# Removing two groups of discarded products from the router stage of a transformer-block kernel

## The reference

```
h = rms_norm(x, norm2_g[l]) * (1.0 + sc2) + sh2
...
logits = (xt @ router_w + router_b).astype(jnp.float32)
top_v, top_e = lax.top_k(logits, TOP_K)          # 4 of 32 experts for each token
gate = jax.nn.softmax(top_v, axis=-1)
...
hb = xb @ w1[e] + b1[e]                          # xb: the tokens of expert e
glu = g * jax.nn.sigmoid(g * SWIGLU_ALPHA)
return ((u + 1.0) * glu) @ w2[e] + b2[e]
```

## Time and profile before

| | |
|---|---|
| median of 3 runs | 2230.92 us (2228.34 to 2231.58) |
| the profiled execution's own time | 2230.52 us |
| its span | 2228.7 us |
| mean granted clock of TensorE | 0.972 |
| PE busy | 2094.6 us (94%) |
| DVE, ACT busy | 701.0 us (31%), 448.4 us (20%) |
| kernel start to the last attention product (L1494) | about 406.5 us |
| router stage, to the first product of expert 0 (L1749) | 406.5 to 442.35 us |
| expert loop | 442.35 to about 1435 us |

### The profile page before, as it was taken

The page is one execution under the profiler, slowest core; times in us unless marked ns, Lnnn a source line. Parts: engine busy times, 40 slices in busy tenths (PEclk is TensorE's granted clock), DMA queues, the critical chain, the costliest instruction groups (busy, mean ns, idle before and its releaser), DMA issues.

```text
span 2228.7 us, 28718 instructions
## 1 busy us (share of the span) xinstructions
PE 2094.6 (94%) x10964; PEld 1204.8 (54%) x10965; DVE 701.0 (31%) x1479; ACT 448.4 (20%) x874; POOL 0.2 (0%) x4
## 2 busy tenths in 40 slices
PE   6999989899989999999999999899999999999997
PEld 3767757433333333333333333376489976648996
DVE  2333223311110111111111111214267753525776
ACT  1322230100000000000000000112245431114543
POOL 0000000000000000000000000000000000000000
PEclk9999989899989999999999999999999999999999
DMA  9254674499978999999999979963166645432652
GB/s 357 89 172 167 227 195 149 186 376 426 424 282 338 425 425 426 425 426 425 426 425 426 424 274 426 366 164 104 29 187 181 184 127 144 139 104 86 196 171 84
DMA packets 189021, 590.95 MB, mean 265 GB/s; under 512 B 10571, under 2 KB 110466, under 8 KB 152996
## 3 DMA queue, kind: packets, MB, share of 16 engines
q1 hardware_dynamic: 186940, 587.68, 70.0%
q10 hardware_dynamic: 2024, 2.46, 0.4%
HBM read 587.48 MB, written 2.62 MB: 265 GB/s over the span
## 4 chain that ended last, share of the span: by engine, by line
PE 76%; DMA 17%; DVE 3%; ACT 2%; issue 1%; SPq 0%; ACTq 0%; DVEq 0%
DMA lower<-in_exp_w 16%; PE psum L1756 15%; PE psum L1941 11%; PE psum L1407 7%; PE psum L1780 6%; PE psum L1953 5%; PE psum L1509 5%; PE psum L1514 5%; PE psum L1541 3%; PE psum L1488 2%; PE psum L1800 2%; PE psum L1724 2%; PE psum L1494 1%; PE psum L1415 1%; PE psum L1749 1%
## 5 line engine op out<-in xcount | busy, mean ns | idle before, releaser
L1756 PE MATMUL psum<-lower,upper 128*64 128x512 f32 x2176 | 487.6, 602 | 25.6 <-DMA lower<-in_exp_w 25.6
L1756 PEld LDWEIGHTS psum<-lower,upper 128*64 128x64 f32 x2176 | 150.9, 137 | 362.4 <-issue 308.2
L1941 PEld LDWEIGHTS psum<-rounded 128*128 128x128 f32 x2112 | 258.6, 189 | 3.4
L1941 PE MATMUL psum<-rounded 128*128 128x256 f32 x2112 | 260.1, 283 | 0.0
L1780 PE MATMUL psum<-upper 128*64 128x512 f32 x1088 | 240.5, 595 | 6.8 <-ACT upper L1176 6.8
L2402 DVE TENSOR_SCALAR upper<-psum 128x512 f32<-128x512 f32 x34 | 23.5, 691 | 692.8 <-PE psum L1756 690.9
L1407 PE MATMUL psum<-upper,lower 128*128 128x256 f32 (+1 forms) x880 | 166.4, 389 | 4.1 <-ACT upper L971 4.1
L1780 PEld LDWEIGHTS psum<-upper 128*64 128x64 f32 x1088 | 75.3, 137 | 149.8 <-issue 137.0
L1407 PEld LDWEIGHTS psum<-upper,lower 128*128 128x128 f32 (+1 forms) x880 | 130.5, 174 | 35.6 <-issue 10.5
L1953 PE MATMUL psum<-rounded 128*128 128x512 f32 x528 | 128.9, 392 | 2.4 <-DVE rounded L2598 2.4
L1171 ACT ACTIVATE upper<-upper 128x512 f32<-128x512 f32 x32 | 20.1, 629 | 496.1 <-DVE upper L2402 496.1
(11 more groups left out here) (374 smaller groups left out, 1794.1 us busy)
## 6 DMA issues: line engine op xcount, KB each, us to landing
lower<-in_exp_w SPq DMA_DIRECT2D x128, 2048.0 KB, 21.4
upper<-in_exp_w SPq DMA_DIRECT2D x128, 1024.0 KB, 20.2
lower<-in_ffn_w_up SPq DMA_DIRECT2D x88, 512.0 KB, 5.3
lower<-in_mod_w SPq DMA_DIRECT2D x12, 2048.0 KB, 10.5
lower<-in_w_in SPq DMA_DIRECT2D x12, 2048.0 KB, 9.7
lower<-in_ffn_w_down SPq DMA_DIRECT2D x44, 512.0 KB, 5.7
lower<-in_odd_w_in SPq DMA_DIRECT2D x8, 2048.0 KB, 11.7
lower<-in_even_w_in SPq DMA_DIRECT2D x7, 2048.0 KB, 11.8
```

What stands on the lines that cost most here:

```text
L1756: ins = pe.matmul(bank[first_bank + r // 2][64 * half:64 * half + 64], rows, w1[k][:, 512 * r:512 * r + 512], start=False, stop=(k == W1_O ...
L1941: ins = pe.matmul(bank[4 + b][:, T * g:T * g + T], w[:, g, k, :], x[:, k, :], start=(k == m == 0), stop=(k == KD - 1 and m == 2))
```

## The change

It deletes the two calls of `keep_busy` in the router stage. All the rest of TensorE's stream, and the streams of the other engines and of the queues, stay as they are.

```diff
@@ -1678,7 +1678,6 @@
                 run_job(n)
 
 
-            keep_busy(bank[7], 6)
             pe.wait_ge(xn2_ready, 1)
             for q in range(4):
                 for kk in range(2):
@@ -1706,7 +1705,6 @@
                         ins = pe.transpose(bank[2 + 2 * i + half][:, P * k:P * k + P],
                                            h2T[:, 4 * half + k, P * i:P * i + P], ident)
                     ins.then_inc(x2_turned, 1)
-            keep_busy(bank[7], 2)
             pe.wait_ge(chosen_ready, 1)
             pe.matmul(bank[7][:, 0:32], ca("tri"), chosen[:, 0, :], start=True, stop=True)
             pe.matmul(bank[7][:, 32:64], ones, chosen[:, 0, :], start=True, stop=False)
```

## The result

The changed kernel is slower: a median of 2233.60 us over 20 runs (2229.36 to 2239.15) against 2227.85 us over 20 runs of the kernel before (2219.77 to 2231.58), a ratio of 1.0029 with a 95% interval of 1.0019 to 1.0038, which is +6.5 us, between +4.2 and +8.5; the two medians themselves lie 5.75 apart. With more runs the kernel before came out 3 us lower than in the three shown ahead of the prediction. Its runs spread over 12 us, so a single pair of runs says nothing here; the profiled pair has spans of 2228.7 and 2234.4 us, 5.7 apart. One execution each of two later variants (without the start's filler, and the same with 3 products in the gap) took 4279 and 3097 us where the others took 2217 to 2235; their ratios leave it out, and its cause is not known.

What follows compares the result with a forecast made beforehand. The prediction took the router stage to lie on the path, with TensorE's granted clock deciding its length and any delay reaching the end. Terms summed to +9.3 us, less 2.4 for rises: +6.9 on 2230.52, 2237.5 us, range 2232.5 to 2241.

Steps and rivals of the forecast that it cites:

- Step 1: Router stage, 16 transposes of L1686: at clock 0.50 they take 0.217 us each instead of 0.119, +1.6 us.
- Step 2: Router logits, 36 instructions: at clock 0.50 throughout they take 7.6 us instead of 4.93, +2.6 us.
- Step 4: L1711 to L1717 after the choice, 12 instructions: at 0.50 if the clock does not rise, +1.2 us.
- Step 5: L1812, 8 instructions: 6.9 us at clock 0.50 instead of 3.63 at 1.00, +3.2 us.
- Steps 6 and 7: L1724 at clock 0.50, +0.5 us; then L1733, its copies, the issue and the loop's bias products, already slow or idle, 0.
- Step 8: Start of expert 0, L1756: a run of about 4.5 us at 0.50 before the clock rises instead of 2.7, +0.9 us.
- the sum taken off for rises: Even chances of a clock rise behind L1686 (saving 2.6 us) and behind L1706 (2.2 us): half of each, 2.4 us off.
- code position: Rival: 16 instructions fewer shift all code behind them, either way by a us or two; chance 0.02.
- both rises: Rival: the clock comes back behind both L1686 and L1706, +4.5 us or +3.6, 2234 to 2235 us; chance 0.18.
- All at 0.50: Rival: no clock rise from the first transposes until expert 0, +9.3 us, 2239.8 up to 2241 us; chance 0.25.
- the clock holds: Rival: the clock outlives the 6.2 us idle before the first transposes, L1711 starts 0.75 us earlier, 2229.8 us; chance 0.05.
- the delay is swallowed: Rival: the weight stream starts ahead of TensorE, so the stage's delay vanishes in later expert-loop waits, 2230.5 us; chance 0.05.

Runs made afterwards that it cites:

- the thin products: Kernel before with the first filler group as 6 products of one row of weights and 512 columns, second group kept: 2231.75 us, ratio 1.0024.
- the short products: Kernel before with both filler groups kept in number but each product 8 columns instead of 512: 2232.75 us, ratio 1.0023.

## Why the prediction was right

The direction, the range and the size held: +6.6 us was forecast over the median then known, +6.5 was measured (5.75 between the medians). The absolute 2237.5 us lies above the measured 2233.60 because the kernel before itself has its median 3 us below that of the three runs. By the steps, against the profiled stage, in which the differences are those of the two profiled executions:

- Where the bound lies: held. No wait in the expert loop swallows the stage's +8.4 us (what came back there, the fifth and the last row of the table, has other causes); SP's next load moved with TensorE, from 449.48 to 460.42, and the waits for weights stayed at 25.7 us in 27 times. SP's queue and TensorE's waits in the changed kernel:

```profile
460.42 0.59 SPq L819 DMA_DIRECT2D upper<-in_exp_b  x1
```

```profile
PE psum L1754 <- DMA lower<-in_exp_w: 25.7, 27, 1.3
```

- Clock down at the first transposes: held in every profile without a dense first group.
- Step 1, transposes: +1.6 forecast, +1.5 measured (to the first logit product, 419.96 - 415.24 = 4.7 against 3.3).
- Step 2, logits: +2.6 at 0.50 throughout, half of it taken off for a rise: +1.3. Measured +1.4 (419.96 to 426.33). That rise, behind the transposes, came in four of the five profiles in which they ran at 0.50 (not behind the thin products), where I had said an even chance; but it saved 1.2 us and not 2.6, since the clock was down again at 422. The two errors cancel.
- Second group: -0.75 forecast, -0.8 measured (431.75 - 426.33 = 5.4 against 6.2).
- Step 4, places: +1.2 forecast, +1.0 measured. Step 5, L1812: +3.2, less 1 us if a rise came; measured +3.5, all at 0.50.
- Steps 6 and 7: +0.5 forecast, +0.3 measured (441.86 to 451.74 against 432.74 to 442.35).
- Step 8, start of expert 0: +0.9 forecast, +1.5 measured: the clock was up only behind 459.4, more than 5.7 us after the first L1754.

**The step that was mis-sized** is the sum taken off for rises, 2.4 us. I priced a rise behind L1706 as saving the places and part of L1812. In both profiles of the changed kernel it came, and in the first it fell into the 2.3 us of idle time that my own step had noted. With nothing to speed up, and the clock back down at 432, it saved 0.2 us of the places and nothing of L1810. With the 1.2 us in the logits the rises saved 1.4 us for the 2.4 taken off. Step 8, mis-sized by another 0.6, does the rest, and the stage came to +8.4 and not +6.9.

**The rival that was under-rated** is code position. I gave it a chance of 0.02 and looked at the branch into the loop, which kept its length (3.89 us before, 4.02 after). The shift acted at the further pass, and gave back 2.4 us of what the stage lost. In the profiled pair another 2.4 came back through earlier clock rises in the expert loop, and 2.5 went the other way before the edit; neither is the change's. Errors of opposite sign made the total look better than the working was: that the size hit so closely is in part luck.

The "both rises" rival shows the same thing: in the changed kernel both rises did come, and the stage was not 4.5 but 8.4 us longer. "All at 0.50" was wrong about the logits, "the clock holds" and "the delay is swallowed" are excluded by the rows above.

One thing stays open. Over all profiles the stage is 46.5, 46.7, 49.5 us with both groups and 53.4, 53.5, 55.1 with neither (or with the short products): +6.4 on average. Less 2.4 for the pass that makes +4.0 for the changed kernel, where the runs say +4.2 to +8.5. Three profiles of each kind are too few to tell whether more than chance is in this.

## What to carry to other kernels

A filler product in a covered wait cost nothing here, and what it buys is read from the granted clock of the stretches behind it, not from its own row in the chain; taking it out is priced by everything that then runs at 0.50, and a clock that comes back in an idle stretch buys nothing. A filler of another shape has to be measured: products with one row of weights took the time and let the clock fall, and products of 8 columns left TensorE idle. And since the code is read in as it runs, the number of instructions ahead of a branch can move a gap of 2 us somewhere else in the kernel, so keep that number the same when one part is tested, as with the products of 8 columns here.

## What the runs showed of the hardware that I had not expected

- The clock rose behind transposes alone. In the changed kernel TensorE had been idle for 6 us at 0.50 or falling to it; then came nothing but the 16 transposes L1685, and at 418.60 the clock was at 1.00. The same came in three more profiles; behind the thin products it did not. The Trainium skill (TensorE: Matmul & The Clock Gate, Part 4: PE-mode transpose) says that they do not count as busy the same way and that the full clock does not engage for them; for these float32 transposes the measurement decides against it.
- Under one-row products that kept TensorE busy without a pause the clock fell to 0.50, some 3 us from their start.
- The gap in the pass grows by some 0.2 us for each instruction that stands ahead of it, from 0.17 us or none at 12 instructions fewer to 3.80 us at 6 more, since a product there takes 0.22 to 0.23 us at 0.50. TensorE goes on 1.3 to 1.5 us after the block of code has landed.
